# One plain channel pair fewer ahead of the seven-product stage of a gated conv-MLP, and a weight ring that begins at another place

## The chip, the cores and the metric

One Trainium2 chip, of which the kernel uses one core. The metric is the device time of one launch in microseconds (us), the median of repeated runs; lower is better. Everything is float32.

## What is computed

A decoder layer on x (1, 1024, 1024): a mixer half, which the change does not touch, and a channel mixer:

```python
h  = rms_norm(x, norm_ffn_pre)                                   # (1024 tokens, 1024)
up = causal_dwconv(h @ w_up, conv_w, taps=3) + conv_b            # w_up: 1024 x 5632
gate, val = split(up, 2)                                         # 2816 channels each
x  = x + rms_norm((silu(gate) * val) @ w_down, norm_ffn_post)    # w_down: 2816 x 1024
```

The 2816 channels are 22 tiles of 128. A *pair* is one tile of gate channels with the tile of value channels of the same number.

## The kernel before, in words

Every float32 product is made of three TensorE matmuls on rounded parts (`product`, L1438 to L1444): high times high, high times low, low times high. So each operand is first rounded by ScalarE into a high part and then subtracted by VectorE into a low part. h transposed lies in `h2hi` and `h2lo` (8 token tiles by 8 k tiles).

Pairs are made in two ways. In a **plain** pair the gate and the value tile are each multiplied with both halves of the tokens: 2 x 2 x 8 k tiles x 3 = 96 matmuls of 512 columns (the loop at L1663). In a **seven-product** pair the same result comes from 7 products (Strassen's scheme with Winograd's sums) over quarters of h and of the pair's weights, each 4 k tiles x 3 = 12 matmuls, together 84 (`seventh`, L1670; the loop over q at L1682). `PLAIN = 3` pairs are plain, and the 19 others (`SEVEN`) are seven-product pairs, q = 0 to 18 for pairs 3 to 21.

The seven products of pair q are here called P1 to P7, in the order in which TensorE issues them. They need:
- the **differences** of h's quarters, four arrays of 128x2048 that are made once. GpSimd adds high and low parts to whole quarters (`whole_quarter`, L581); VectorE combines them (L1331, L1335, L1336, L1343); ScalarE rounds (`round_difference(i)`, L842); VectorE takes the low part (`low_difference(i)`, L1299). P2, P3, P5 and P7 read the differences 0, 1, 2 and 3 (`r_split` counts them).
- the weight **entries** (q, 0) to (q, 3), per pair: raw blocks or sums of them. GpSimd makes the sums (`sum_weights`, L586, three instructions, after the low part of entry (q-1, 2)), ScalarE rounds (`round_entry`, L848), VectorE takes the low part (`low_entry`, L1305, counted by `u_split`). P1 and P4 read entry 0, P2 and P5 entry 1, P3 and P6 entry 2, P7 entry 3.
- copies and additions of partial products: ScalarE copies the results of P1, P2 and P3 out of PSUM (`keep(q, 0..2)`, L867), since P3 adds onto the bank of P1 and P5 onto that of P3; VectorE adds them elsewhere (`fold(q, 0..2)`, L1318), and P7 waits for the second of these.

After its products a pair is convolved: ScalarE starts gate and value (`start_gate`, `start_value`), VectorE adds the taps (`gate_taps`, `value_taps`, two instructions each), ScalarE takes SiLU, VectorE multiplies (`gate_value`).

Entries go round a **ring** of six places (`entry`, L358): two in `w2hi`/`w2lo`, two in a quarter of `h2hi`/`h2lo` that only plain pairs and the differences read, two in `whi`/`wlo`, which the plain pairs' weights use before. Entries (0, 2) and (0, 3) lie in the h2 quarter, so they wait until all plain pairs are done (L853 and L854).

No planner sets the order: each engine runs its own program in the order in which the code is written. ScalarE's order around the change is at L900 to L931, VectorE's at L1329 to L1370, TensorE's at L1663 to L1703, GpSimd's at L605 to L610, and SyncE's, which loads weights and stores results, at L488 to L491: `load_pair(p)` waits for two `w_split` if pair p-2 is plain, otherwise for the four `u_split` of pair p-2, and `save_act(p-3)` follows it in the same queue.

Of the kernel before, what the change touches and what calls it, by code (L numbers as in the profile page):

```python
# [21 lines left out]
ACT = mybir.ActivationFunctionType  # L22
# [11 lines left out]
NF = DFF // P  # L34
# [13 lines left out]
UP0 = W_O0 + KD  # L48
# [13 lines left out]

PLAIN = 3
SEVEN = NF - PLAIN
W_SPLIT_DOWN = UP0 + 2 * PLAIN
RING = 6

ENTRY_LAST = (4, 5, 6, 7)  # L70


def build(nc, consts, x, norm_mix_pre, w_in, pool_w, pool_scale, conv_w, attn_sinks, w_o,
# [10 lines left out]
    with ctx:  # L84
# [20 lines left out]
        whi = alloc(ctx, "whi", [P, SPLIT, DM], F32R)  # L105
# [18 lines left out]
        h2hi = alloc(h2, "h2hi", [P, NT, KD, P], F32R)  # L124
        h2lo = alloc(h2, "h2lo", [P, NT, KD, P], F32R)
# [58 lines left out]
        w2hi = alloc(x2_, "w2hi", [P, 2, DM], F32R)  # L184
        w2lo = alloc(x2_, "w2lo", [P, 2, DM], F32R)
        w_sums = alloc(x2_, "w_sums", [P, 4, HALF])
        yg = alloc(x2_, "yg", [P, 2, SEQ])
        yv = alloc(x2_, "yv", [P, 2, SEQ])
# [16 lines left out]
        def banks(b, n=2):  # L205
            return ps[:, b:b + n, :].rearrange("p b c -> p (b c)")
# [16 lines left out]
        def ffn_tap(j, f):  # L223

            return par_b[:, bass.ds(f, 1)] if j == 2 else par_a[:, bass.ds(2 * NF * j + f, 1)]

        def ffn_bias(f):
            return par_b[:, bass.ds(2 * NF + f, 1)]
# [13 lines left out]
        act_saved = [sem("act_saved0"), sem("act_saved1")]  # L242
# [56 lines left out]
        up_done = sem("up_done")  # L299
        neg_ready = sem("neg_bias_ready")  # L300
        quartered = sem("h2_quarters_added")
# [9 lines left out]
        yg_started = sem("gate_started")  # L311
        yv_started = sem("value_started")
        silu_done = sem("silu_done")
        up_freed = sem("up_convolved")
        act_ready = sem("act_ready")
# [41 lines left out]

        def entry(q, i, lo):  # L358

            at = (4 * q + i) % RING  # L360
            if at < 2:
                return (w2lo if lo else w2hi)[:, at, :].rearrange("p (h c) -> p h c", h=2)
            if at < 4:
                t = 4 + 2 * (at - 2)
                return (h2lo if lo else h2hi)[:, t:t + 2, 0:4, :].rearrange("p t k c -> p t (k c)")
            return (wlo if lo else whi)[:, at - 4, :].rearrange("p (h c) -> p h c", h=2)

        def raw_blocks(pair):
# [10 lines left out]
        def _(sp):  # L379
# [39 lines left out]
            def load_pair(p):  # L419
                for val in range(2):  # L420
                    n = UP0 + 2 * p + val
                    if p - 2 < PLAIN:
                        sp.wait_ge(w_split, n - RAW + 1)
# [132 lines left out]
        def _(pool):  # L556
# [29 lines left out]
            def sum_weights(q):  # L586

                pair = PLAIN + q
                raw = raw_blocks(pair)
# [38 lines left out]
        def _(act):  # L628
            def round_weight(base, q, hi, slot):

                n = base + RAW * q
                act.wait_ge(landed[base % RAW], 16 * (base // RAW + 1 + q))
                act.activation(hi[:, slot, :], wraw[:, base % RAW, :], ACT.Copy)\  # L633
                   .then_inc(w_rounded, 1)
# [180 lines left out]
                    round_ring(UP0 + t - 4)  # L815
            round_h(2 * NT - 1, h2hi)

            def plain_step(p):

                j = p % 2  # L820
                act.wait_ge(up_done, 2 * p + 1)
                if p + 1 < PLAIN:
                    round_weight(UP0 + 2 * p + 2, 0, whi, 0)
                if p >= 2:
                    act.wait_ge(act_ready, p - 1)
                act.activation(yg[:, j, :], banks(4 * j), ACT.Identity, bias=ffn_bias(p),
                               scale=ffn_tap(2, p)).then_inc(yg_started, 1)
                act.wait_ge(up_done, 2 * p + 2)
                if p + 1 < PLAIN:
                    round_weight(UP0 + 2 * p + 3, 0, whi, 1)  # L830
                if p >= 2:
                    act.wait_ge(act_saved[j], 16 * (p // 2))
                act.activation(yv[:, j, :], banks(4 * j + 2), ACT.Identity,
                               bias=ffn_bias(p + NF), scale=ffn_tap(2, p + NF))\
                   .then_inc(yv_started, 1)
                start_silu(p)

            def start_silu(p):
                act.wait_ge(up_freed, 2 * p + 1)
                act.activation(yg[:, p % 2, :], yg[:, p % 2, :], ACT.Silu).then_inc(silu_done, 1)  # L840

            def round_difference(i):  # L842
                act.wait_ge(r_made, i + 1)
                act.activation(r_hi[i][:, :, :, :].rearrange("p t k c -> p (t k c)"),
                               r_full[i][:, :, :].rearrange("p t c -> p (t c)"),
                               ACT.Copy).then_inc(r_rounded, 1)

            def round_entry(q, i):  # L848
                pair = PLAIN + q
                before = 4 * q + i - RING  # L850
                if before >= 0:
                    act.wait_ge(seven_done, 7 * (before // 4) + ENTRY_LAST[before % 4])
                elif (4 * q + i) % RING >= 2:  # L853
                    act.wait_ge(up_done, 2 * PLAIN)  # L854
                if i in (0, 3):
                    n = UP0 + 2 * pair + (i == 3)
                    act.wait_ge(landed[n % RAW], 16 * (n // RAW + 1))
                    raw = raw_blocks(pair)
                    src = raw[:, 0:2, :] if i == 0 else raw[:, 3:4, :]
                else:  # L860
                    act.wait_ge(summed, 3 * q + (1 if i == 1 else 3))
                    src = w_sums[:, 0:2, :] if i == 1 else w_sums[:, 2:4, :]
                out = entry(q, i, False)
                act.activation(out[:, 0:1, :] if i == 3 else out, src, ACT.Copy)\
                   .then_inc(u_rounded, 1)
# [31 lines left out]
            for q in x2_saved:  # L897
                act.wait_ge(q, 16 * NT // 2)
            act.wait_ge(neg_ready, 1)
            plain_step(0)  # L900
            plain_step(1)
            round_difference(0)
            round_entry(0, 0)
            round_entry(0, 1)
            round_difference(1)
            plain_step(2)
            round_difference(2)
            round_entry(0, 2)
            round_entry(0, 3)
            round_difference(3)  # L910
            for q in range(SEVEN):
                if q >= 1:
                    start_value(q - 1)
# [64 lines left out]
        def _(dve):  # L978
# [261 lines left out]
            for t in range(NT):  # L1240
                rows = x2b[:, t % 2, :]
                i = NT + 2 * t
# [29 lines left out]
            def gate_taps(p):  # L1272
                dve.wait_ge(yg_started, p + 1)
                add_taps(yg[:, p % 2, :], banks(4 * (p % 2)), p)

            def value_taps(p):
                dve.wait_ge(yv_started, p + 1)
                add_taps(yv[:, p % 2, :], banks(4 * (p % 2) + 2), p + NF)

            def gate_value(p, sign):  # L1280

                dve.wait_ge(up_freed, 2 * p + 2)
                dve.wait_ge(silu_done, p + 1)
                dve.scalar_tensor_tensor(yv[:, p % 2, :], yv[:, p % 2, :], sign, yg[:, p % 2, :],
                                         ALU.mult, ALU.mult).then_inc(act_ready, 1)

            def plain_step(p):
                if p + 1 < PLAIN:
                    low_weight(UP0 + 2 * p + 2, 0, whi, wlo, 0)
                gate_taps(p)  # L1290
                if p + 1 < PLAIN:
                    low_weight(UP0 + 2 * p + 3, 0, whi, wlo, 1)
                value_taps(p)
                gate_value(p, 1.0)
# [4 lines left out]
            def low_difference(i):  # L1299
                dve.wait_ge(r_rounded, i + 1)  # L1300
                dve.tensor_tensor(r_lo[i][:, :, :, :].rearrange("p t k c -> p t (k c)"), made(i),
                                  r_hi[i][:, :, :, :].rearrange("p t k c -> p t (k c)"),
                                  ALU.subtract).then_inc(r_split, 1)

            def low_entry(q, i):  # L1305
                dve.wait_ge(u_rounded, 4 * q + i + 1)
                hi, lo = entry(q, i, False), entry(q, i, True)
                raw = raw_blocks(PLAIN + q)
                if i == 0:
                    src = raw[:, 0:2, :]  # L1310
                elif i == 3:
                    src, hi, lo = raw[:, 3:4, :], hi[:, 0:1, :], lo[:, 0:1, :]
                else:
                    dve.wait_ge(summed, 3 * q + 3)
                    src = w_sums[:, 2 * i - 2:2 * i, :]
                dve.tensor_tensor(lo, src, hi, ALU.subtract).then_inc(u_split, 1)  # L1316
# [12 lines left out]
            plain_step(0)  # L1329
            dve.wait_ge(quartered, 2)  # L1330
            dve.tensor_tensor(made(0), made(0), made(2), ALU.subtract).then_inc(r_made, 1)  # L1331
            plain_step(1)
            dve.wait_ge(r_made, 1)
            dve.wait_ge(quartered, 3)
            finish_step(dve.tensor_tensor(made(2), made(1), made(2), ALU.subtract))  # L1335
# [7 lines left out]
            dve.scalar_tensor_tensor(made(3), made(1), -1.0, made(3), ALU.mult, ALU.subtract)\  # L1343
               .then_inc(r_made, 2)
            low_difference(1)
            plain_step(2)
            low_difference(2)
            low_entry(0, 2)
            low_entry(0, 3)
            low_difference(3)  # L1350
            for q in range(SEVEN):
                if q >= 1:
                    value_taps(PLAIN + q - 1)
# [61 lines left out]
            for t in range(4):  # L1415
                i, slot = 3 * NT + 4 + t, t % 2
# [373 lines left out]
```

## Time and profile before

| | |
|---|---|
| median of 3 runs | 1002.41 us (999.76 to 1004.15) |
| the profiled execution, its own time | 1003.03 us |
| its span in the trace | 1001.2 us |
| mean granted TensorE clock | 0.994 of full |
| TensorE (PE) busy | 983.2 us, 98% |
| VectorE (DVE) busy | 613.3 us, 61% |
| ScalarE (ACT) busy | 407.8 us, 41% |
| GpSimd (POOL) busy | 158.2 us, 16% |

Times in the rows are microseconds from the start of the span. A row of a timeline gives the start, the duration, the engine, the line of the kernel, the operation, what it writes and reads with its shape, and how many instructions are merged; in square brackets stands how long the engine had been idle before, and which instruction released it. A matmul's duration includes its way through the array, so matmuls overlap; what counts is the distance between their starts. L1441 to L1443 are the three matmuls of every product. A helper's line serves many calls: L1301 is every `low_difference`, L1316 every `low_entry`, L1326 every `fold`, L1262 and L1264 the taps, L864 every `round_entry`, L844 every `round_difference`, L877 every `keep`.

### The profile page before, as it was taken

Reading aid. Unit: us, or ns where it says so; the run is one execution under the profiler, and the core shown is the slowest. Engines: PE = TensorE matmul, PEld = TensorE weight load, DVE = VectorE, ACT = ScalarE, POOL = GpSimd, SP = SyncE. Lnnn points to the kernel's source line nnn. Section 1 sums busy time; section 2 is a strip of 40 time slices with the busy share of each in tenths; the row PEclk is TensorE's granted clock in tenths of the full one; section 3 lists DMA queues with packets and bytes.
Section 4 is the critical chain, followed back from the end, with each engine's and each line's share of the span. In section 5 each row is a group of like instructions: output and inputs, shape, how many; then the busy total and the mean of one; then the engine's idle time right before and its main releaser. Section 6 shows DMA issues by size and latency. Waiting matters only on the chain.

```text
span 1001.2 us, 11938 instructions
## 1 busy us (share of the span) xinstructions
PE 983.2 (98%) x4580; PEld 810.0 (81%) x4580; DVE 613.3 (61%) x641; ACT 407.8 (41%) x624; POOL 158.2 (16%) x143
## 2 busy tenths in 40 slices
PE   8999999999999998999999999999999999999997
PEld 7988777777888887888888888888887888888886
DVE  4646786664555579777677677677665333344454
ACT  5525444443343335444445445445433323333342
POOL 2200000000111832332242232232200000000001
PEclk9999999999999999999999999999999999999999
DMA  6511110016223321232223223223315444455553
GB/s 221 154 49 37 43 43 22 25 61 209 85 85 104 86 84 47 80 93 86 75 79 90 84 66 102 85 64 105 105 64 191 155 139 144 157 191 197 182 175 126
DMA packets 84911, 104.90 MB, mean 105 GB/s; under 512 B 3849, under 2 KB 63489, under 8 KB 84865
## 3 DMA queue, kind: packets, MB, share of 16 engines
q1 hardware_dynamic: 84737, 104.20, 31.9%
q8 instruction: 31, 0.51, 0.2%
q14 instruction: 15, 0.12, 0.0%
q0 software_dynamic: 128, 0.07, 0.0%
HBM read 84.33 MB, written 19.92 MB: 104 GB/s over the span
## 4 chain that ended last, share of the span: by engine, by line
PE 91%; DVE 3%; DMA 2%; ACT 1%; POOL 1%; issue 1%; SPq 0%; DVEq 0%; POOLq 0%; ACTq 0%
PE ps L1441 29%; PE ps L1442 29%; PE ps L1443 29%; PE ps L1451 1%; PE ps L1549 1%; PE ps L1572 1%; DMA wraw<-in_w_in 1%; PE ps L1550 1%; PE ps L1558 1%; PE ps L1576 1%; DMA wraw<-in_w_o 1%; DMA act_in<-act_dram 0%; DVE hlo L992 0%; PE ps L1587 0%; DVE w2lo L1316 0%
## 5 line engine op out<-in xcount | busy, mean ns | idle before, releaser
L992 DVE TENSOR_TENSOR wlo<-wraw,whi 128x1024 fp32r<-128x1024 f32 x60 | 75.8, 1265 | 138.1 <-ACT whi L633 137.8
L633 ACT ACTIVATE whi<-wraw 128x1024 fp32r<-128x1024 f32 x60 | 63.4, 1058 | 173.4 <-PE ps L1443 169.3
L1441 PE MATMUL ps<-whi,ahi 128*128 128x512 f32 x320 | 124.6, 389 | 1.6 <-DVE alo L1269 1.6
L1443 PE MATMUL ps<-whi,alo 128*128 128x512 f32 x320 | 124.5, 389 | 0.0
L1442 PE MATMUL ps<-wlo,ahi 128*128 128x512 f32 x320 | 124.5, 389 | 0.0
L1441 PE MATMUL ps<-hhi,whi 128*128 128x512 f32 (+1 forms) x256 | 96.4, 376 | 2.3 <-DVE hlo L1010 2.3
L1442 PE MATMUL ps<-hlo,whi 128*128 128x512 f32 (+1 forms) x256 | 93.7, 366 | 0.0
L1443 PE MATMUL ps<-hhi,wlo 128*128 128x512 f32 (+1 forms) x256 | 93.7, 366 | 0.0
L563 POOL TENSOR_SCALAR meansq<-sumsq 128x1 f32<-128x1 f32 x28 | 7.6, 272 | 526.7 <-ACT x2b L804 241.7
L595 POOL TENSOR_TENSOR w_sums<-wraw 128x1024 f32<-128x1024 f32 x19 | 46.7, 2459 | 255.2 <-DVE h2lo L1316 103.4
L1441 PEld LDWEIGHTS ps<-whi,ahi 128*128 128x128 f32 x320 | 60.1, 188 | 14.4 <-DVE alo L1269 2.0
L1443 PEld LDWEIGHTS ps<-whi,alo 128*128 128x128 f32 x320 | 60.1, 188 | 12.6
L1442 PEld LDWEIGHTS ps<-wlo,ahi 128*128 128x128 f32 x320 | 60.1, 188 | 12.4
L1441 PE MATMUL ps<-h2hi,whi 128*128 128x512 f32 x168 | 65.5, 390 | 0.0
L1442 PE MATMUL ps<-h2lo,whi 128*128 128x512 f32 x168 | 65.4, 389 | 0.0
L1443 PE MATMUL ps<-h2hi,wlo 128*128 128x512 f32 x168 | 65.4, 389 | 0.0
L1441 PEld LDWEIGHTS ps<-hhi,whi 128*128 128x128 f32 x256 | 49.1, 192 | 10.0 <-DVE hlo L1010 2.7
L1443 PEld LDWEIGHTS ps<-hhi,wlo 128*128 128x128 f32 x256 | 49.1, 192 | 7.6
L1442 PEld LDWEIGHTS ps<-hlo,whi 128*128 128x128 f32 x256 | 49.1, 192 | 7.4 <-issue 0.5
L1441 PE MATMUL ps<-hhi,mhi 128*128 128x512 f32 x128 | 51.3, 401 | 2.2 <-DVE hlo L992 2.2
L1442 PE MATMUL ps<-hlo,mhi 128*128 128x512 f32 x128 | 50.6, 395 | 0.0
L1443 PE MATMUL ps<-hhi,mlo 128*128 128x512 f32 x128 | 50.5, 394 | 0.0
(196 smaller groups left out, 2215.8 us busy)
## 6 DMA issues: line engine op xcount, KB each, us to landing
wraw<-in_ffn_w_up SPq DMA_DIRECT2D x44, 512.0 KB, 5.1
wraw<-in_ffn_w_down SPq DMA_DIRECT2D x44, 512.0 KB, 3.4
act_dram<-yv SPq DMA_DIRECT2D x22, 512.0 KB, 2.6
act_in<-act_dram SPq DMA_DIRECT2D x42, 256.0 KB, 3.5
wraw<-in_w_in SPq DMA_DIRECT2D x14, 512.0 KB, 4.0
xin<-in_x SPq DMA_DIRECT2D x8, 512.0 KB, 4.3
wraw<-in_w_o SPq DMA_DIRECT2D x8, 512.0 KB, 3.3
xres<-in_x SPq DMA_DIRECT2D x8, 512.0 KB, 4.2
```

What stands on the lines that cost most here:

```text
L595: pool.tensor_tensor(w_sums[:, 0:2, :], raw[:, 0:4:3, :], raw[:, 2:3, :].broadcast_to([P, 2, HALF]), ALU.add)\
L633: act.activation(hi[:, slot, :], wraw[:, base % RAW, :], ACT.Copy)\
L992: dve.tensor_tensor(lo[:, slot, :], wraw[:, base % RAW, :], hi[:, slot, :], ALU.subtract).then_inc(w_split, 1)
L1441: pe.matmul(acc, w_hi, x_hi, start=first, stop=False, skip_group_check=looped)
L1442: pe.matmul(acc, w_hi, x_lo, start=False, stop=False, skip_group_check=looped)
L1443: return pe.matmul(acc, w_lo, x_hi, start=False, stop=last, skip_group_check=looped)
L1451: last = pe.transpose(ps[:, b + k // 4, (k % 4) * P:(k % 4 + 1) * P], rows[:, k * P:(k + 1) * P], ident)
L1549: pe.matmul(acc, q, k_hi[:, kv, keys], start=True, stop=False)
L1550: last = pe.matmul(acc, q, k_lo[:, kv, keys], start=False, stop=True)
L1558: last = pe.transpose(ps[:, 6, i * P:(i + 1) * P], prob[:, u % 2, i, :], ident)
L1572: last = pe.matmul(acc, v_tok[:, b, cols], pt_cur[:, heads, :].rearrange("p h q -> p (h q)"), start=True, stop=b == 0)
L1576: last = pe.matmul(acc, v_tok[:, b - 1, cols], pt_prev[:, heads, :].rearrange("p h q -> p (h q)"), start=False, stop=True)
```

## The change

`PLAIN` goes from 3 to 2, so pair 2 becomes a seven-product pair and q runs from 0 to 19, for pairs 2 to 21. The ring is entered at its third place (`RING_FROM = 2`), and the names of the first two pairs of places are exchanged: entries (0, 0) and (0, 1) still lie in `w2`, (0, 2) and (0, 3) now in `whi`/`wlo`, and the first to lie in the h2 quarter are (1, 0) and (1, 1). Entry (0, 2) waits for the first three of the plain pairs' four tiles, entry (0, 3) for all four, those of q = 1 also for the whole quarters. ScalarE's and VectorE's programs around the transition are written in another order: the work of the last plain pair (now pair 1) is split up and put among the differences and entries.

```diff
-PLAIN = 3
+PLAIN = 2
 SEVEN = NF - PLAIN
 W_SPLIT_DOWN = UP0 + 2 * PLAIN
 RING = 6
+RING_FROM = 2
@@ def entry(q, i, lo)
-            at = (4 * q + i) % RING
+            at = (4 * q + i + RING_FROM) % RING
             if at < 2:
-                return (w2lo if lo else w2hi)[:, at, :].rearrange("p (h c) -> p h c", h=2)
+                t = 4 + 2 * at
+                return (h2lo if lo else h2hi)[:, t:t + 2, 0:4, :].rearrange("p t k c -> p t (k c)")
             if at < 4:
-                t = 4 + 2 * (at - 2)
-                return (h2lo if lo else h2hi)[:, t:t + 2, 0:4, :].rearrange("p t k c -> p t (k c)")
+                return (w2lo if lo else w2hi)[:, at - 2, :].rearrange("p (h c) -> p h c", h=2)
@@ ScalarE: plain_step(p) becomes start_plain(p, val), one half of it, and start_silu(p)
+            def start_plain(p, val):
+                j, y = p % 2, (yg, yv)[val]
+                act.wait_ge(up_done, 2 * p + val + 1)
                 if p + 1 < PLAIN:
-                    round_weight(UP0 + 2 * p + 2, 0, whi, 0)
...
+                    round_weight(UP0 + 2 * p + 2 + val, 0, whi, val)
+                act.activation(y[:, j, :], banks(4 * j + 2 * val), ACT.Identity,
+                               bias=ffn_bias(p + val * NF), scale=ffn_tap(2, p + val * NF))\
+                   .then_inc((yg_started, yv_started)[val], 1)
@@ def round_entry(q, i)
-                elif (4 * q + i) % RING >= 2:
-                    act.wait_ge(up_done, 2 * PLAIN)
+                elif 4 * q + i >= 2:
+                    act.wait_ge(up_done, 2 * PLAIN - (4 * q + i == 2))
+                    if 4 * q + i >= 4:
+                        act.wait_ge(quartered, 2)
@@ ScalarE, the order
-            plain_step(0)
-            plain_step(1)
+            start_plain(0, 0)
+            start_plain(0, 1)
+            start_silu(0)
             round_difference(0)
             round_entry(0, 0)
             round_entry(0, 1)
             round_difference(1)
-            plain_step(2)
             round_difference(2)
+            start_plain(1, 0)
             round_entry(0, 2)
+            round_difference(3)
+            start_plain(1, 1)
             round_entry(0, 3)
-            round_difference(3)
+            start_silu(1)
@@ VectorE, the order
             plain_step(0)
             dve.wait_ge(quartered, 2)
             dve.tensor_tensor(made(0), made(0), made(2), ALU.subtract).then_inc(r_made, 1)
-            plain_step(1)
...
             low_difference(1)
-            plain_step(2)
+            gate_taps(1)
             low_difference(2)
             low_entry(0, 2)
+            low_difference(3)
             low_entry(0, 3)
-            low_difference(3)
+            value_taps(1)
+            gate_value(1, 1.0)
```

## Rows read from the trace of the kernel before

**Rows 1.** The page, the chain that ended last: shares of the span by engine.

```profile
PE 91%; DVE 3%; DMA 2%; ACT 1%; POOL 1%; issue 1%; SPq 0%; DVEq 0%; POOLq 0%; ACTq 0%
```

**Rows 2.** Timeline of PE: pair 1's end, products of q = 0, two of q = 1.

```profile
364.35 0.39 PE L1441 MATMUL ps<-h2hi,whi 128*128 128x512 f32 x1
...
386.11 0.39 PE L1441 MATMUL ps<-h2hi,w2hi 128*128 128x512 f32 x1
...
395.05 0.77 PE L1441 MATMUL ps<-r_hi,h2hi 128*128 128x512 f32 x1 [3.35 <-ACT yg L877]
...
399.47 0.39 PE L1441 MATMUL ps<-h2hi,w2hi 128*128 128x512 f32 x1
...
410.38 0.39 PE L1441 MATMUL ps<-h2hi,whi 128*128 128x512 f32 x1
...
416.41 0.50 PE L1441 MATMUL ps<-r_hi,w2hi 128*128 128x512 f32 x1 [0.43 <-ACT yg L877]
```

**Rows 3.** Busy time by stretch, q = 0: stretch, length, PE, PEld, DVE, ACT, POOL, clock, DMA.

```profile
386.11:410.38 24.27, 20.92 (x86) 16.89 (x84) 21.46 (x15) 12.77 (x14) 12.00 (x5) 0.93 0.22 66
```

**Rows 4.** Timeline of DVE, from the first difference to the folds of q = 0.

```profile
355.87 2.30 DVE L992 TENSOR_TENSOR wlo<-wraw,whi 128x1024 fp32r<-128x1024 f32 x1
...
372.87 2.29 DVE L1336 SCALAR_TENSOR_TENSOR r_full<-r_full 128x2048 f32<-128x2048 f32 x1
375.08 2.28 DVE L1301 TENSOR_TENSOR r_lo<-r_full,r_hi 128x2048 fp32r<-128x2048 f32 x1
377.28 1.22 DVE L1316 TENSOR_TENSOR w2lo<-wraw,w2hi 128x1024 fp32r<-128x1024 f32 x1
...
379.55 2.28 DVE L1343 SCALAR_TENSOR_TENSOR r_full<-r_full 128x2048 f32<-128x2048 f32 x1
381.75 2.28 DVE L1301 TENSOR_TENSOR r_lo<-r_full,r_hi 128x2048 fp32r<-128x2048 f32 x1
383.96 1.27 DVE L1262 SCALAR_TENSOR_TENSOR yg<-ps,par_a,yg 128x1023 f32<-128x1023 f32 x1
...
390.18 1.22 DVE L1284 SCALAR_TENSOR_TENSOR yv<-yv,yg 128x1024 f32<-128x1024 f32 x1
...
395.26 4.45 DVE L1301 TENSOR_TENSOR r_lo<-r_full,r_hi 128x2048 fp32r<-128x2048 f32 x1
...
404.95 1.22 DVE L1316 TENSOR_TENSOR w2lo<-w_sums,w2hi 128x1024 fp32r<-128x1024 f32 x1
...
406.69 2.60 DVE L1316 TENSOR_TENSOR w2lo<-wraw,w2hi 128x512 fp32r<-128x512 f32 x1
409.21 0.69 DVE L1326 TENSOR_TENSOR ps<-ps,yv 128x512 f32<-128x512 f32 x1
```

**Rows 5.** Timeline of POOL: weight sums of q = 0, 1 and 2.

```profile
353.87 3.22 POOL L599 TENSOR_TENSOR w_sums<-w_sums,wraw 128x512 f32<-128x512 f32 x1
357.17 2.16 POOL L602 TENSOR_TENSOR w_sums<-w_sums,wraw 128x512 f32<-128x512 f32 x1
394.91 2.66 POOL L595 TENSOR_TENSOR w_sums<-wraw 128x1024 f32<-128x1024 f32 x1 [35.58 <-DVE h2lo L1316]
...
406.34 2.40 POOL L595 TENSOR_TENSOR w_sums<-wraw 128x1024 f32<-128x1024 f32 x1 [3.23 <-DVE w2lo L1316]
408.82 1.62 POOL L599 TENSOR_TENSOR w_sums<-w_sums,wraw 128x512 f32<-128x512 f32 x1
```

**Rows 6.** Timeline of ACT: one of each kind of instruction at the transition.

```profile
375.20 1.92 ACT L844 ACTIVATE r_hi<-r_full 128x2048 fp32r<-128x2048 f32 x1 [3.85 <-DVE r_full L1336]
377.02 1.19 ACT L826 ACTIVATE yg<-ps,par_b 128x1024 f32<-128x1024 f32 x1
...
390.17 1.04 ACT L864 ACTIVATE h2hi<-w_sums 128x1024 fp32r<-128x1024 f32 x1
391.11 0.62 ACT L864 ACTIVATE h2hi<-wraw 128x512 fp32r<-128x512 f32 x1
...
394.38 1.06 ACT L877 ACTIVATE yg<-ps 128x512 f32<-128x512 f32 x2
```

**Rows 7.** DMA issues, 380 to 440: queue, KB each, median us to landing.

```profile
wraw<-in_ffn_w_up SPq DMA_DIRECT2D x6, 512.0 KB, 4.8
```

More of the change, by code:

```diff
@@ L816, in _ @@
             round_h(2 * NT - 1, h2hi)
-            def plain_step(p):
-                j = p % 2
-                act.wait_ge(up_done, 2 * p + 1)
+            def start_plain(p, val):
+                j, y = p % 2, (yg, yv)[val]
+                act.wait_ge(up_done, 2 * p + val + 1)
                 if p + 1 < PLAIN:
-                    round_weight(UP0 + 2 * p + 2, 0, whi, 0)
[L824 to L836, printed above, removed]
+                    round_weight(UP0 + 2 * p + 2 + val, 0, whi, val)
+                act.activation(y[:, j, :], banks(4 * j + 2 * val), ACT.Identity,
+                               bias=ffn_bias(p + val * NF), scale=ffn_tap(2, p + val * NF))\
+                   .then_inc((yg_started, yv_started)[val], 1)
             def start_silu(p):
```

## The prediction

> **What bounds the kernel now.** I read the chain that ended last first: TensorE holds 91% of it [rows 1], so a removed matmul is time saved, unless TensorE then waits. Next comes its timeline for the places where it does wait [rows 2]. From 399.47 (P4 of q = 0) to 410.38 (P1 of q = 1) lie 48 matmuls with no gap: 0.2273 us apiece, so 12 take 2.73 us, a seven-product pair 19.1, a plain pair 21.8. The transition is not at this pace: q = 0 takes 24.27 us, P3 starts only at 395.05 after 3.35 us idle, released by a ScalarE copy, and P3 of q = 1 starts at 416.41 where 24 matmuls after 410.38 would give 415.84. From 386.11 to 416.41 are 30.3 us for 108 matmuls that need 24.55, a loss of 5.75 us. The 12 matmuls of P3 after the idle time take 4.42 us in place of 2.73, as the granted clock of this stretch is 0.93 [rows 3]: part of it ran at 1.2 GHz, not 2.4. Last I read VectorE, GpSimd and ScalarE there [rows 4 to 6], because they decide when P3 may go. After 416.41 TensorE shows no other gap until the down stage, so it suffices to ask when P3 of q = 1 starts, with the other engines in the same positions behind it.
>
> **What it removes.** One plain pair becomes a seven-product pair, 96 to 84 matmuls: -2.73 us. That holds if the transition loses as much as today. Behind P3 of q = 1 the changed kernel has one pair more than before, 19.1 us, so its time is (its start of that P3) - 416.41 + 19.1. Equal time needs that start at 397.3.
>
> **What it moves.** Pair 1 ends at 364.35 [rows 2]; P1 of q = 0 could start there, 21.8 us earlier than today. But the differences and entries do not come 21.8 us earlier: VectorE, ScalarE and GpSimd have the same work to do with one plain pair less as cover. I follow VectorE from 355.87, where the first difference has been made and today a low weight of pair 2 starts [rows 4]; up to there nothing changes.
>
> VectorE and GpSimd take turns. GpSimd's L599 at 353.87 takes 3.22 us where the one at 408.82 takes 1.62, and VectorE's 512-column entry at 406.69 lasts 2.60 us and ends when GpSimd's L595 (406.34 + 2.40) has gone by plus about 0.6 [rows 4, 5]: one waits for the other's whole instruction.
> - The two combinations L1335 and L1336 (2.2 us from start to start, 372.87 to 375.08) now come at 355.87. The first waits for GpSimd's L599 to 357.1 and ends at 359.2; GpSimd's last sum (about 1.3 alone) goes to 360.4, the second combination ends at 362.55.
> - Low difference 0 (2.2), entries (0, 0) and (0, 1) (1.14 each), L1343 (2.2), low difference 1 (2.2) by the pitches of rows 4: entry (0, 0) is ready at 365.9, (0, 1) at 367.0, the last combination at 369.2, low difference 1 at 371.4. So P1 starts at 366.0 instead of 364.35, P2 follows, and both end at 371.4.
> - ScalarE waits for the last combination (369.2) before difference 2 (1.9) [rows 6], then starts the gate of pair 1 (1.2): 372.3. Behind it are queued entry (0, 2) (1.0), difference 3 (1.9), the value of pair 1 (1.2), entry (0, 3) (0.6), SiLU (taken as 1.0, the same size as an entry), entry (1, 0) (1.0) and only then keep (0, 0) (0.6), which ends at 379.0. P3 waits for it.
> - VectorE: gate taps 372.3 to 374.9 (2.6: two of 1.3), low difference 2 to 377.1, entry (0, 2) ready at 378.25, which P3 needs too. P3 therefore starts at 379.1, after 7.7 us of idle time; today that is 3.35.
> - Low difference 3 issues at 378.17, just ahead of GpSimd's L595 for the next pair (it waits for entry (0, 2)), and should take 2.3, not the 4.45 of the row at 395.26, whose turn came after a short entry had let GpSimd in. Then GpSimd 380.4 to 382.7, entry (0, 3) to 383.3, value taps to 385.8, and the product of gate and value waits for GpSimd's third sum and ends at 387.3 (alone 1.22). Entries (1, 0) and (1, 1) to 389.6, fold 0 to 390.2, entry (1, 2) from 390.1, fold 1 until 392.0, entry (1, 3) behind GpSimd's L595, fold 2 at 394.4 (4.26 after entry (1, 2) started, as from 404.95 to 409.21).
> - TensorE meanwhile: P3 at the slow pace to 383.5, P4, P5, P6 to 391.7, P7 waits for fold 1 to 392.0, P1 and P2 of q = 1 would be done at 400.2.
> - From fold 2 to P3 of q = 1 it is 7.2 us today (409.21 to 416.41: gate start, taps, SiLU, entry, keep). 394.4 + 7.2 = 401.6. That P3 waits 1.4 us.
>
> **The sum.** 401.6 - 416.41 + 19.1 = +4.3; unrounded it is +4.2. By losses: 1.6 (P1) + 7.7 (P3) + 1.7 (clock) + 0.3 (P7) + 1.4 (next P3), with rounding 12.6 against 5.75 today, less the 2.73. 1003.03 + 4.2 = 1007.2 for the profiled execution; that one lies 0.6 above the median 1002.41, so I forecast 1006.6. A measurement of this kernel can tell about 0.5%, 5.0 us, from no change: this is +0.42%.
>
> **At nothing.** The ring's new order alone: the places have the same size and the instructions that use them the same shape; with 20 pairs the last users of `whi` are again the third and fourth entries of the last but one pair, so the down stage starts as now. Its cover, if the places were wrong, would be a wait of each entry for a product 6 entries back; steady pairs show no such wait on TensorE, and the distance is unchanged. SyncE's queue: `load_pair(4)` now waits for entry (0, 3) (383.3) and holds back the store of pair 1, ready at 387.3 anyway. Its two loads land 4.8 us after issue [rows 7], about 389.3, ahead of GpSimd's 391.4; nobody needs the sum before 400. The half clock after P3's idle time costs nothing beyond the 1.7, as P7 and the next P3 wait for VectorE anyway; without it the time would be the same.
>
> **The unknown: who takes a turn.** Low difference 3 beside GpSimd: 2.3 at least (it is ahead), 4.45 at most (the row at 395.26). At 4.45 GpSimd's second sum also goes ahead of entry (0, 3), which is ready at 385.0; the product follows at 388.75 in place of 387.3, so everything behind is 1.45 later: +5.7. I take 2.3, because the issue order differs from that row's. The first combination has 2.3 and 4.48 as ends (its neighbour before 355.87 ran twice its time beside GpSimd), I have 3.4: 1.1 either way.
>
> A rule speaks to this. The Trainium skill (SBUF — State Buffer, Who interferes with whom) says that whichever engine issues first holds the shared pair of ports for its whole instruction. By it low difference 3 goes first and the result is +4.2; by the nearest row it would be +5.7. The 512-column entry of 2.60 agrees with a lock and not with sharing, which would about double its time to 1.3.
>
> **Rivals.**
> (a) *VectorE loses its turns and the transition costs more* (slower side). Place: low difference 3, then the product and entry (1, 3). Price +1.45, together +5.7, 1008.1; it decides if GpSimd's L595 is issued before low difference 3 starts, a margin of 0.2 us. For it: that is what happened at 395.26. Against: the order there. A wait on ScalarE's list of seven items ahead of keep (0, 0) can add to it. Chance 0.30.
> (b) *The transition loses no more than today*: P3's 3.35 us, the slow 12 matmuls. Then -2.73, 999.7. It needs VectorE's chain 7 us shorter than I follow it. For: three instruction groups of pair 2's plain work are gone. Against: they are not in the chain above. Chance 0.06.
> (c) *All waits vanish*, -2.73 - 5.75 = -8.5, 993.9: only if keep (0, 0) came by 371. Chance 0.05.
> (d) *TensorE stays at 1.2 GHz* after the longer idle time up to P3 of q = 1: 84 matmuls at 4.42/12 = 0.368 from 379.1 give 410.0, +12.7, 1015.1. For it only that the idle time doubles; the 12 matmuls after 395.05 were back at full pace by P4. Chance 0.03.
> (The Trainium skill, TensorE: Matmul & The Clock Gate, HAM oscillation, describes kernels that swing between the two levels when matmul groups are spaced by waits; that would be (d).)
> That the change does not do what it says has no room here: the counts are constants.
>
> **How the numbers follow.** Forecast +4.2: chance 0.56, within 0.5%. Faster by over 0.5%: (c), 0.05. Slower: (a) and (d), 0.33. Within: the forecast and (b), 0.62. The range goes 5 us below the forecast, to 1001.5, for a shorter first combination and the scatter of the runs (999.76 to 1004.15), and up to 1010.5, which takes in (a) with the same scatter. It leaves out (b), (c), (d).
>
> **What the changed trace would show.** 12 matmuls fewer, 4568 in place of 4580. P1 of q = 0 about 1.6 us after pair 1's end, then P3 7 to 8 us late, released by a keep on ScalarE then a half-pace stretch of 12 matmuls; a fold ahead of P7; P3 of q = 1 near 401.6. VectorE without idle time over 1.2 us between 355.9 and 395. Low difference 3 of 2.3 us would confirm the turn taken, 4.45 would give (a). I would be wrong if P3 started before 375, or if a gap appeared on TensorE later than 402, which none of this accounts for.

## The result, and the profile after

The changed kernel took 1005.91 us (median of 9 runs, 1004.79 to 1008.31) against 1002.02 us for the one before in the same session (9 runs, 999.76 to 1004.33). The ratio is 1.0040, 95% interval 1.0029 to 1.0052: slower by 0.4%, 3.9 us of the medians, less than the 0.5% that was named as the bound of "no change". The forecast was +4.2 us and 1006.6 us.

The page of the changed kernel, span and busy time by engine:

```profile
span 1003.3 us, 11939 instructions
PE 979.1 (98%) x4568; PEld 806.1 (80%) x4568; DVE 618.6 (62%) x646; ACT 412.3 (41%) x629; POOL 163.6 (16%) x146
```

There are 4568 matmuls, 12 fewer than before, and TensorE is 4.1 us less busy, yet the span is 2.1 us longer. The two spans cannot be compared directly. Both kernels are the same up to the last transposes of the mixer half, and that point lies at different times in different executions. So I use the start of those eight transposes as a **mark** for all traces. Timelines of PE, before and after, the mark:

```profile
326.69 1.06 PE L1451 MATMUL ps<-cst,hrow_c 128*128 128x128 f32 x8 [0.51 <-DVE hrow_c L1254]
```

```profile
325.21 1.06 PE L1449 MATMUL ps<-cst,hrow_c 128*128 128x128 f32 x8 [0.52 <-DVE hrow_c L1251]
```

The execution shown of the changed kernel had been 1.48 us quicker to that point. Timeline of PE of the changed kernel at the transition: P1 and P3 of q = 0, P4 of q = 0, P1 and P3 of q = 1:

```profile
364.56 0.47 PE L1439 MATMUL ps<-h2hi,w2hi 128*128 128x512 f32 x1 [1.53 <-DVE w2lo L1313]
...
377.64 0.77 PE L1439 MATMUL ps<-r_hi,whi 128*128 128x512 f32 x1 [7.36 <-ACT yg L871]
...
382.11 0.39 PE L1439 MATMUL ps<-h2hi,w2hi 128*128 128x512 f32 x1
...
393.05 0.39 PE L1439 MATMUL ps<-h2hi 128*128 128x512 f32 x1
...
399.77 0.50 PE L1439 MATMUL ps<-r_hi,w2hi 128*128 128x512 f32 x1 [1.12 <-ACT yg L871]
```

These are the rows that answer to [rows 2]. From the mark to P3 of q = 1 it is 74.56 us; before it was 89.72. One more pair of 19.04 us follows (the distance of the folds of two steady pairs, 84 matmuls at 0.2267), so the transition accounts for 74.56 + 19.04 - 89.72 = +3.9 us, the size of the difference of the medians. From the mark to the end of the span it is 678.1 us against 674.5 before, +3.6: the only other wait of TensorE until there that differs is the one at the start of the down stage, 1.32 us in place of 1.62. TensorE idles 1.5 us ahead of P1, 7.4 ahead of P3 and 1.1 ahead of the next P3, and P3's 12 matmuls take 4.47 us. P7 starts at 390.26, 65.05 us after the mark, right behind P6 and 0.1 us after fold 1 has ended (389.45 + 0.69). Busy time by stretch of the changed kernel (columns as in [rows 3]), around P3:

```profile
377.60:382.10 4.50, 4.46 (x12) 3.56 (x13) 4.50 (x3) 0.43 (x1) 4.42 (x2) 0.60 0.01 4
```

The granted clock is 0.60 there: most of it ran at 1.2 GHz.

### VectorE and GpSimd after

Timeline of DVE of the changed kernel, from the first of the two combinations to fold 2 of q = 0, to be read beside [rows 4]:

```profile
354.51 3.27 DVE L1331 TENSOR_TENSOR r_full<-r_full 128x2048 f32<-128x2048 f32 x1
357.82 3.27 DVE L1332 SCALAR_TENSOR_TENSOR r_full<-r_full 128x2048 f32<-128x2048 f32 x1
...
370.84 1.28 DVE L1259 SCALAR_TENSOR_TENSOR yg<-ps,par_a,yg 128x1023 f32<-128x1023 f32 x1 [0.88 <-ACT yg L826]
...
375.56 1.22 DVE L1313 TENSOR_TENSOR wlo<-w_sums,whi 128x1024 fp32r<-128x1024 f32 x1
376.69 2.29 DVE L1298 TENSOR_TENSOR r_lo<-r_full,r_hi 128x2048 fp32r<-128x2048 f32 x1
378.89 2.87 DVE L1313 TENSOR_TENSOR wlo<-wraw,whi 128x512 fp32r<-128x512 f32 x1
...
389.45 0.69 DVE L1323 TENSOR_TENSOR ps<-ps,yg 128x512 f32<-128x512 f32 x1
390.05 2.59 DVE L1313 TENSOR_TENSOR w2lo<-wraw,w2hi 128x512 fp32r<-128x512 f32 x1
392.56 0.69 DVE L1323 TENSOR_TENSOR ps<-ps,yv 128x512 f32<-128x512 f32 x1
```

Timeline of POOL of the changed kernel, the third sum of q = 0 and the first of q = 1:

```profile
355.71 3.22 POOL L603 TENSOR_TENSOR w_sums<-w_sums,wraw 128x512 f32<-128x512 f32 x1
376.94 4.27 POOL L596 TENSOR_TENSOR w_sums<-wraw 128x1024 f32<-128x1024 f32 x1 [18.01 <-DVE wlo L1313]
```

VectorE has one idle time, 0.88 us, in 38 us. The turns can be read off: GpSimd's sum issued at 355.71 (1.3 us alone) gets its turn when VectorE's combination has ended at 357.8, and ends 1.15 us later; VectorE's next combination takes 3.27 us, not 2.29, because that sum is ahead of it. Low difference 3, issued at 376.69, takes 2.29: it is ahead of GpSimd's sum of 376.94, which takes 4.27 instead of 2.39, and entry (0, 3) behind both takes 2.87 instead of 0.7. That decides between the two prices of the prediction: the turn was taken, not lost.

### The profile page after: what moved, and what is told of

Its sections match the earlier page's. It is cut to its first block, busy times and chain, and to the rows that moved or that the text cites. A ratio compares the mean times of both kernels' runs of the same rounds, so it can differ in the third digit from the quotient of the medians.

```text
span 1003.3 us, 11939 instructions
## 1 busy us (share of the span) xinstructions
PE 979.1 (98%) x4568; PEld 806.1 (80%) x4568; DVE 618.6 (62%) x646; ACT 412.3 (41%) x629; POOL 163.6 (16%) x146
## 4 chain that ended last, share of the span: by engine, by line
PE 89%; DVE 6%; DMA 2%; ACT 1%; issue 1%; SPq 0%; POOL 0%; DVEq 0%; POOLq 0%; ACTq 0%
PE ps L1439 28%; PE ps L1441 28%; PE ps L1440 28%; PE ps L1449 1%; PE ps L1547 1%; PE ps L1570 1%; DMA wraw<-in_w_in 1%; PE ps L1548 1%; PE ps L1556 1%; DVE r_lo L1298 1%; PE ps L1574 1%; DMA wraw<-in_w_o 1%; DVE w2lo L1313 0%; DMA act_in<-act_dram 0%; DVE r_full L1328 0%
## 5 line engine op out<-in xcount | busy, mean ns | idle before, releaser
L989 DVE TENSOR_TENSOR wlo<-wraw,whi 128x1024 fp32r<-128x1024 f32 x58 | 72.4, 1249 | 133.1 <-ACT whi L634 132.8
L634 ACT ACTIVATE whi<-wraw 128x1024 fp32r<-128x1024 f32 x58 | 61.3, 1059 | 159.0 <-PE ps L1441 154.1
L596 POOL TENSOR_TENSOR w_sums<-wraw 128x1024 f32<-128x1024 f32 x20 | 50.7, 2537 | 253.4 <-DVE wlo L1313 99.4
L1440 PEld LDWEIGHTS ps<-wlo,ahi 128*128 128x128 f32 x320 | 60.1, 188 | 12.4
L1439 PE MATMUL ps<-h2hi,whi 128*128 128x512 f32 x140 | 54.6, 390 | 0.0
L1440 PE MATMUL ps<-h2lo,whi 128*128 128x512 f32 x140 | 54.5, 389 | 0.0
L1441 PE MATMUL ps<-h2hi,wlo 128*128 128x512 f32 x140 | 54.5, 389 | 0.0
```

What stands on the lines that cost most here:

```text
L596: pool.tensor_tensor(w_sums[:, 0:2, :], raw[:, 0:4:3, :], raw[:, 2:3, :].broadcast_to([P, 2, HALF]), ALU.add)\
L989: dve.tensor_tensor(lo[:, slot, :], wraw[:, base % RAW, :], hi[:, slot, :], ALU.subtract).then_inc(w_split, 1)
L1439: pe.matmul(acc, w_hi, x_hi, start=first, stop=False, skip_group_check=looped)
L1440: pe.matmul(acc, w_hi, x_lo, start=False, stop=False, skip_group_check=looped)
L1441: return pe.matmul(acc, w_lo, x_hi, start=False, stop=last, skip_group_check=looped)
```

## The experiments

Each is told by three numbers: the distance from the mark to P3 of q = 0 and to P3 of q = 1, and the ratio to the kernel before with its interval. With two plain pairs, 19.04 us are added before it is compared with three. The edits are shown shortened, some of them in words.

| kernel | mark to P3, q = 0 | mark to P3, q = 1 | ratio | median, us |
|---|---|---|---|---|
| before | 68.36 | 89.72 | 1 | 1001.5 to 1003.0 by session |
| changed | 52.43 | 74.56 | 1.0040 [1.0029, 1.0052] | 1005.91 |
| e1, ring of before | 52.41 | 74.55 | 1.0036 [1.0022, 1.0050] | 1005.24 |
| e2, keep (0, 0) earlier | 51.69 | 74.52 | 1.0039 [1.0025, 1.0053] | 1005.90 |
| e3, VectorE longer | 52.41 | 76.91 | 1.0057 [1.0038, 1.0075] | 1007.72 |
| e4, filler matmuls | 52.38 | 74.55 | 1.0040 [1.0025, 1.0054] | 1005.95 |
| e5, quarters on VectorE | 45.60 | 67.72 | 0.9967 [0.9953, 0.9981] | 999.02 |
| e6, reordered | no gap | 65.45 | 0.9950 [0.9932, 0.9968] | 998.49 |
| e7, folds first | no gap | 62.13 | 0.9914 [0.9889, 0.9938] | 993.56 |
| e10, the same again | no gap | 62.13 | 0.9896 [0.9874, 0.9918] | 992.49 |
| e8, three plain, quarters on VectorE | 68.37 | 89.71 | 0.9983 [0.9971, 0.9995] | 1001.15 |
| e11, the same again | 68.36 | 89.71 | 1.0003 [0.9988, 1.0018] | 1003.44 |
| e9, three plain, clean | 65.54 | 84.69 | 0.9933 [0.9913, 0.9953] | 996.30 |
| e12, changed again | 52.42 | 74.54 | 1.0054 [1.0035, 1.0073] | 1007.79 |

### Does the ring's order cost anything?

```diff
-RING_FROM = 2
+RING_FROM = 0
 places 0, 1: w2; places 2, 3: the h2 quarter; places 4, 5: whi/wlo
 entries (0, 2), (0, 3): wait for all plain tiles and two whole quarters
 first down weights: wait for P4 and P5 of the last pair
```

> The changed kernel with the ring of the kernel before (first two places in w2, then the h2 quarter, then whi/wlo), so entries (0, 2) and (0, 3) lie in the h2 quarter and wait for all four plain tiles; the first down weights then wait for P4 and P5 of the last pair. Theory (the loss is VectorE's and ScalarE's chain at the transition, the ring's order costs nothing): P3 of q = 0 and P3 of q = 1 within 0.3 us of the changed kernel's 377.6 and 399.8, total within noise of its 1005.9, +3.9 to before. Rival (the ring's order is part of the loss): total 2 us or more below the changed kernel's.

P3 of q = 1 comes 74.55 us after the mark, 0.01 us from the changed kernel. The ring's order costs nothing at this transition: entries (0, 2) and (0, 3) were late anyway. At the end of the stage it leaves a wait of 0.30 us on TensorE at 753.54 that the changed kernel does not have.

### Is it the queue ahead of keep (0, 0)?

```diff
             round_difference(3)
+            keep(0, 0)
             start_plain(1, 1)
...
-                for which in range(3):
+                for which in range(q == 0, 3):
```

> The changed kernel with keep (0, 0) moved ahead of the value start of pair 1 on ScalarE, past four instructions. Theory (VectorE's chain up to fold 2 sets the time, TensorE's idle time ahead of P3 does not): P3 of q = 0 starts 0.8 us earlier, 376.8 in place of 377.6, now released by entry (0, 2); P3 of q = 1 stays at 399.8 and the total at +3.9 to before. Rival (the queue ahead of the copy is the cost): P3 of q = 1 and the total come earlier by the same 0.8 us or more.

Timeline of PE, P3 of q = 0 and of q = 1:

```profile
378.70 0.77 PE L1440 MATMUL ps<-r_hi,whi 128*128 128x512 f32 x1 [6.63 <-DVE wlo L1314]
...
401.53 0.50 PE L1440 MATMUL ps<-r_hi,w2hi 128*128 128x512 f32 x1 [0.81 <-ACT yg L871]
```

P3 is now released by VectorE's entry and comes 0.74 us earlier (51.69 after the mark). P3 of q = 1 comes 0.04 us earlier. Idle time ahead of P3 was shortened and the kernel did not get faster: the copy that the profile names as releaser is not what sets the time. The fair comparison is e12 below, the changed kernel in an execution in which P3's 12 matmuls took 5.3 us as they did here: of the 0.73 us gained ahead of P3, 0.66 came back as idle time ahead of the next P3 (0.81 us against 0.15).

### Is it VectorE's chain?

```diff
             value_taps(1)
+            for _ in range(2):
+                finish_step(dve.tensor_tensor(gain_a[:, :], banks(4), h2lo_tile_0, ALU.add))
             gate_value(1, 1.0)
```

> The changed kernel with two more VectorE instructions of 128x1024 (about 1.3 us each, one input in PSUM, result not used) between the value taps of pair 1 and its product, so after P3 of q = 0 has been released. Theory (VectorE's chain from there to fold 2 sets the time): P3 of q = 0 stays at 377.6, P7 of q = 0 and P3 of q = 1 come 2.6 us later, total +6.5 to before. Rival (what counts is TensorE's idle time ahead of P3): +3.9 as now, the 2.6 us lie beside TensorE's work.

Timelines of DVE and PE: the added pair, then P3 and P7 of q = 0 and P3 of q = 1:

```profile
384.40 2.47 DVE L1349 TENSOR_TENSOR gain_a<-ps,h2lo 128x1024 f32<-128x1024 f32 x2
```

```profile
377.86 0.77 PE L1443 MATMUL ps<-r_hi,whi 128*128 128x512 f32 x1 [7.38 <-ACT yg L871]
...
392.85 0.47 PE L1443 MATMUL ps<-r_hi,whi 128*128 128x512 f32 x1 [1.51 <-issue]
...
402.36 0.50 PE L1443 MATMUL ps<-r_hi,w2hi 128*128 128x512 f32 x1 [1.09 <-ACT yg L871]
```

The two instructions took 2.5 us, P3 of q = 0 stayed (52.41), and P3 of q = 1 came 2.35 us later, with P7 now waiting 1.5 us. The profile names no releaser for P7 ("issue"), but P7 starts 0.10 us after fold 1 has ended (392.06 + 0.69 on VectorE), and it is the same 0.10 us in e4 and e6. Time added to VectorE behind P3's release goes into the total almost in full. The measured ratio, 1.0057, has the changed kernel's within its interval, so here the trace shows it and the median only leans that way.

### Is it the half clock?

```diff
+                if q == 0:
+                    for _ in range(30):
+                        pe.matmul(bank g0, a weight of entry (0, 0), h2hi quarter, start=True, stop=True)
                 pe.wait_ge(kept, 3 * q + 1)
```

> The changed kernel with 30 matmuls of 512 columns whose result is overwritten, between P2 and P3 of q = 0: 6.8 us of work in the idle time, so that the granted clock does not fall. Theory: P3 takes 2.7 us in place of 4.5, but P7 still waits for fold 1 on VectorE and P3 of q = 1 for the copy, so the total stays at +3.9 to before (within 0.4). Rival (the half clock is part of the loss): total 1.7 us below the changed kernel's, +2.2 to before.

Timelines of PE and DVE: the fillers, P3 and P7 of q = 0, P3 of q = 1, then fold 1:

```profile
372.53 7.00 PE L1692 MATMUL ps<-h2hi,w2hi 128*128 128x512 f32 x30
...
379.99 0.50 PE L1439 MATMUL ps<-r_hi,whi 128*128 128x512 f32 x1 [0.46 <-ACT yg L871]
...
392.65 0.47 PE L1439 MATMUL ps<-r_hi,whi 128*128 128x512 f32 x1 [1.48 <-issue]
...
402.16 0.50 PE L1439 MATMUL ps<-r_hi,w2hi 128*128 128x512 f32 x1 [1.11 <-ACT yg L871]
```

```profile
391.86 0.69 DVE L1323 TENSOR_TENSOR ps<-ps,yg 128x512 f32<-128x512 f32 x1
```

P3's 12 matmuls ran at full pace (2.86 us in place of 4.47), and what they gained turned into the 1.48 us that P7 waits for fold 1. P7 starts 65.04 us after the mark, P3 of q = 1 74.55, both where they were. In e12, the changed kernel once more, the half clock lasted longer: the 12 matmuls of P3 took 5.3 us, and P3 of q = 1 was again at 74.54 with only 0.15 us of idle time ahead of it. So the half clock was free here, but with little to spare:

```profile
380.08 0.76 PE L1439 MATMUL ps<-r_hi,whi 128*128 128x512 f32 x1 [7.36 <-ACT yg L871]
...
402.20 0.50 PE L1439 MATMUL ps<-r_hi,w2hi 128*128 128x512 f32 x1 [0.15 <-ACT yg L871]
```

> The changed kernel itself beside the three others: ratio 1.004 to before.

Its ratio, 1.0054, has an interval from 1.0035 that overlaps the first, so +4 to +5.5 us is what the ratios of two sessions give (the medians of this one lie 6.2 us apart). The two traces agree within 0.3 us from the mark to the end of the span (678.3 and 678.1), so the rest is not at the transition; where it comes from is open.

One number joins the three tests: from the start of fold 2 to P3 of q = 1 it is 7.19 to 7.21 us in the kernel before, in the changed one and in e1 to e6 and e12, whatever TensorE does in between.

### Shortening the chain: the quarters on VectorE

```diff
 GpSimd
-            for i, out in ((0, 0), (3, 2), (2, 1), (1, 3)):
-                whole_quarter(i, out)
+            pool.wait_ge(quartered, 4)
 VectorE, ahead of plain_step(0)
+            dve.wait_ge(ht_split, 2 * NT)
+            dve.wait_ge(wo_done, NT)
+            for i, out in ((0, 0), (3, 2), (2, 1), (1, 3)):
+                whole_quarter(i, out)
```

> The changed kernel with the four whole quarters added by VectorE (four instructions of 128x2048, 2.2 us each, in its idle time from 328.6 on) and not by GpSimd, whose weight sums begin behind them; every order otherwise as in the changed kernel. Theory: the instructions after the first difference come 6.8 us earlier (second combination done at 354.3 in place of 361.1), P1 of q = 0 follows pair 1 with no gap at 362.9, P3 starts at 370.9 after some 2.5 us idle, P3 of q = 1 at 393.0; total 6.8 us below the changed kernel's, 2.9 below before (ratio 0.997). Rival (ScalarE's queue or the waits for up_done set the time): P3 of q = 1 moves by less than 3 us.

Timeline of DVE, the four quarters, and of PE, both P3:

```profile
328.19 8.90 DVE L1323 TENSOR_TENSOR r_full<-h2hi,h2lo 128x2048 f32<-128x2048 f32 x4
```

```profile
370.36 0.47 PE L1442 MATMUL ps<-r_hi,whi 128*128 128x512 f32 x1 [2.34 <-ACT yg L865]
...
392.48 0.50 PE L1442 MATMUL ps<-r_hi,w2hi 128*128 128x512 f32 x1 [1.09 <-ACT yg L865]
```

Four quarters took 8.9 us on VectorE, in idle time; in the kernel before, GpSimd took 20.3 us for them and held up VectorE's instructions of the first plain pair. The Trainium skill (GPSIMD Engine Reference, Elementwise — side-by-side cycle accounting) gives 4497 against 2293 ns for an add of 2048 float32 elements per partition; here VectorE's took 2.29 us each, and GpSimd's 4.60 for the first, beside which VectorE was idle (328.61 to 337.12 in the changed kernel), and up to 5.6 for the later ones, beside a working VectorE. The trace agrees with the page within some 2%. P1 follows pair 1 without a gap, P3 of q = 1 is 6.84 us earlier than in the changed kernel (expected 6.8), and the ratio is 0.9967.

### Reordering for the deadlines

```diff
 VectorE (e6)
+ made(0) between the gate and value work of pair 0
+ low_entry(0, 0), made(3), low_difference(0), low_entry(0, 1), low_difference(1), low_entry(0, 2),
+ gate_taps(1), value_taps(1), low_entry(0, 3), low_difference(2), low_difference(3), gate_value(1)
 ScalarE (e6)
+ ... start_plain(1, 0), round_entry(0, 2), round_difference(2), round_difference(3),
+ start_plain(1, 1), round_entry(0, 3), keep(0, 0), start_silu(1)
 VectorE (e7), q = 0, in place of the loop's order
+ fold(0, 0), gate_value(1), fold(0, 1), low_entry(1, 0), low_entry(1, 1), fold(0, 2),
+ low_entry(1, 2), gate_taps(2), low_entry(1, 3)
 ScalarE (e7): keep(1, 0) ahead of start_silu(2)
```

> As the quarters on VectorE, and both engines' programs reordered up to the loop over q: VectorE makes all differences first, takes entry (0, 2) before and low differences 2 and 3 after the taps of pair 1; ScalarE copies keep (0, 0) ahead of SiLU of pair 1. Theory: P1, P2 and P3 of q = 0 follow pair 1 with no gap (P3 at 368.3), P7 waits 2.7 us for fold 1 on VectorE, P3 of q = 1 starts at 391.6; total 8.2 us below the changed kernel's, 4.3 below before (0.996). Rival (P3's idle time is the cost, so that removing it brings all): P3 of q = 1 at 388, 12 us below the changed kernel's.

Timeline of PE of e6, P7 of q = 0 and P3 of q = 1:

```profile
383.17 0.47 PE L1447 MATMUL ps<-r_hi,whi 128*128 128x512 f32 x1 [1.79 <-issue]
...
392.69 0.50 PE L1447 MATMUL ps<-r_hi,w2hi 128*128 128x512 f32 x1 [1.09 <-ACT yg L865]
```

P3's idle time is gone and, as the theory had it, that alone is not all: P7 waits 1.8 us (expected 2.7) and the next P3 1.1. P3 of q = 1 is 9.1 us earlier than in the changed kernel, where 8.2 was expected and 12 by the rival.

> As the reordered kernel, and at q = 0 VectorE does fold 0 ahead of the product of pair 1, fold 1 ahead of entry (1, 0), fold 2 ahead of entry (1, 2) and the gate taps ahead of entry (1, 3); ScalarE does keep (1, 0) ahead of the SiLU of pair 2. Theory: no wait of TensorE is left from pair 1 to P3 of q = 1 at 387.4, the loss of the transition is below 1 us, total 12 us below the changed kernel's and 8.5 below before, 993.5 (ratio 0.9915). If only part of the waits goes, what is left shows as a gap ahead of P7 or P3.

Timeline of PE of e7, P1 of q = 0 and P3 of q = 1, and its busy time by stretch:

```profile
362.50 0.39 PE L1457 MATMUL ps<-h2hi,w2hi 128*128 128x512 f32 x1
...
386.98 0.39 PE L1457 MATMUL ps<-r_hi,w2hi 128*128 128x512 f32 x1
```

```profile
330.00:362.00 32.00, 32.00 (x143) 26.50 (x142) 31.86 (x19) 17.70 (x14) 7.70 (x3) 1.00 0.16 50
362.00:381.00 19.00, 19.00 (x85) 15.73 (x85) 18.93 (x16) 9.07 (x12) 5.01 (x3) 1.00 0.27 84
```

24.48 us for 108 matmuls, 0.2267 apiece: no loss is left, the clock stays at 1.00, and TensorE is busy without a break while VectorE is busy 18.93 of 19 us. 993.56 us, ratio 0.9914 where 0.9915 was expected; again with more rounds:

> The kernel with the folds first once more, with more rounds: ratio 0.9915 to before, 8.5 us below, and 12.4 us below the changed kernel timed beside it.

992.49 us, 0.9896 [0.9874, 0.9918]. This version beats both kernels. It lies below the one before by 8.6 us by the traces, by 9.4 and 9.1 us by the medians of the two sessions, and by 8.6 and 10.4 by their ratios.

### Three plain pairs with the same treatment

> The kernel before (three plain pairs) with the quarters added by VectorE in the same way, its orders otherwise kept. Theory: there P3 of q = 0 is released by ScalarE's copy, which stands in its queue behind everything that follows pair 2's end at 386.1, and none of that waits for the differences; so P3 stays 3.4 us idle and the total is that of before within 0.5 us (ratio 1.000). Rival (late differences are what cost there as well): P3 and the total 3 us earlier or more.

Only the quarters' move, applied to the kernel before. Both P3 are where they were, to 0.01 us, but the ratio of 0.9983 was not explained by that. Hence the repetition:

> The kernel before with only the quarters moved to VectorE once more, since its first ratio of 0.9983 was 1.8 us lower than its trace explains. Theory (the transition is unchanged): ratio 0.9995, within 0.1% of 1. Rival (the quarters on VectorE gain time elsewhere): 0.998 again.

1.0003, and from the mark to the end of the span both executions take 0.2 us less than the kernel before (674.3 and 674.4 against 674.5). So the first ratio is put down to scatter, and an interval that leaves out 1 by 0.05% is no proof of a gain. The loss of the changed kernel rests on firmer ground: e1, e2, e4 and e12 all show it again. With three plain pairs VectorE's late quarters are covered, and P3 waits for ScalarE's copy alone.

```diff
 the kernel before, quarters on VectorE, and at the transition
 ScalarE: gate start of pair 2, differences 2 and 3, entry (0, 2), value start, entry (0, 3), keep(0, 0), SiLU
 VectorE: gate_taps(2), low_difference(2), low_difference(3), low_entry(0, 2), value_taps(2),
          low_entry(0, 3), then the folds as in e7
```

> Three plain pairs and the ring of before, with the quarters on VectorE and both engines' programs reordered at the transition in the manner of the kernel with the folds first. Theory (with no wait at the transition the seven-product pair is worth its 12 matmuls): no gap on TensorE from pair 2 to P3 of q = 1, total 5.8 us below before (ratio 0.994) and 2.7 us above the same with two plain pairs. Rival (plain pairs and seven-product pairs differ by more than their matmuls): any other distance to that kernel than 2 to 3.5 us.

Timelines of PE (P3 of q = 0), of ACT (rounding of entry (0, 2)) and of DVE (low differences 2 and 3, then the low part of that entry):

```profile
390.60 0.47 PE L1465 MATMUL ps<-r_hi,h2hi 128*128 128x512 f32 x1 [0.53 <-DVE h2lo L1321]
```

```profile
384.67 1.06 ACT L858 ACTIVATE h2hi<-w_sums 128x1024 fp32r<-128x1024 f32 x1 [0.71 <-PE ps L1467]
```

```profile
384.83 4.48 DVE L1306 TENSOR_TENSOR r_lo<-r_full,r_hi 128x2048 fp32r<-128x2048 f32 x2
389.24 1.22 DVE L1321 TENSOR_TENSOR h2lo<-w_sums,h2hi 128x1024 fp32r<-128x1024 f32 x1
```

Three plain pairs lose 0.8 us at this transition (25.28 us for the 108 matmuls), and P3 waits for entry (0, 2). Two things come together there. The entry lies in the h2 quarter, so ScalarE rounds it only after pair 2 has ended, at 384.67. And its low part stands in VectorE's program behind low differences 2 and 3, which P3 does not need, and so starts at 389.24. One low difference takes 2.2 us, so with the entry between the two it would by estimate have been ready at 388.2, ahead of the 389.9 at which P2 ends, and P3 would have had no wait in the old ring either; no run tries it. By the traces two plain pairs are 84.69 - 62.13 - 19.04 = 3.5 us better, 2.7 for the 12 matmuls and 0.8 for this wait; by the medians 3.8 in the same session, just outside the 2 to 3.5 us that the expectation allowed, and 2.7 against e7. The expectation of no gap failed by this one wait, and whether the new ring order has any worth of its own is not shown.

## Why the prediction was right

**The saving**, -2.73 us for 12 matmuls: right. It follows from the pace, 12 x 0.2267 us, and of the 3.5 us between the traces of e9 and e7 it is what remains when e9's loss of 0.8 is taken off.

**VectorE's chain from 355.87**: right to some tenths. With 1.48 us added for the earlier mark, the second combination ended at 362.6 (predicted 362.55), P3 of q = 0 started at 379.1 (379.1), low difference 3 took 2.29 us (2.3), fold 2 issued at 394.0 (394.4), P3 of q = 1 started at 401.25 (401.6). The 0.4 us too much came from the product of pair 1, for which I had it wait for GpSimd's third sum; that sum had ended by then. For the same reason P7 did not wait for a fold, as I had said the trace would show: fold 1 ended 0.1 us ahead of it, and the 0.3 us priced for it did not appear. The loss of the transition was 12.4 us against 12.6. That the median came out within 0.7 us of the forecast is in part luck: the changed kernel's own median moved by 1.9 us from one session to the other.

**Which wait counts.** The prediction had both TensorE's idle time ahead of P3 and VectorE's chain to fold 2 in one list of losses, though it said that the half clock costs nothing because the later waits are VectorE's. That was right and the list invites the wrong reading: e2 shortened the largest entry of it and nothing came of it, e4 removed the 1.7 us and P7 waited instead. Each loss on TensorE is real time, but in this kernel the sum of them is fixed by VectorE's chain to fold 2 and the 7.2 us behind it.

**Rival (a)**, lost turns, +5.7: the trace speaks against it, the turn was taken. Its price cannot be seen. **(b)** and **(c)**, no more waits than today: wrong for this change, and both to be had with other orders: e5 and e7 lie at -3.0 and -8.6 us by the traces, as (b) and (c) had priced them (-2.7 and -8.5). **(d)**, the clock staying low: after 7.4 us of idle time it was at 1.2 GHz for some 3.6 us in one execution and 5.7 in another (below), not to the end.

**At nothing**: the ring's order (e1) cost nothing, as said. SyncE's loads did not show as a wait of TensorE anywhere after the mark.

## What to carry to other kernels

A block of independent work is also cover for what must be ready after it. Before shortening it, add up the engines that prepare the next stage and compare with what is left; here 21.8 us of cover went for 2.7 us of matmuls. Follow the chain past the largest gap: the releaser named at the gap (a ScalarE copy) could be moved without effect, and what counted was the engine without idle time. And give setup work to an engine in its idle time rather than to a slower one that shares its turns: this turned +3.9 us into -3.0, and ordering by deadline into -8.6.

## What the runs showed of the hardware

- The length of the half-clock stretch after the same idle time of 7.36 to 7.38 us was not the same: P3's 12 matmuls took 4.47 us in the changed kernel's first trace and 5.25, 5.26 and 5.11 in e12, e1 and e3, 2.73 at full pace. Over the first 8.2 us from P3 the granted clock was 0.78 in the first and 0.65 in e12, so with the two levels it was at 1.2 GHz for 2 x 0.22 x 8.2 = 3.6 us and 2 x 0.35 x 8.2 = 5.7 us. P3 of q = 1 started 74.56, 74.54 and 74.55 us after the mark in the first, e12 and e1.
- VectorE and GpSimd alternate by whole instructions with both inputs in SBUF, in every row looked at (2.29 us alone, 3.27 or 4.48 behind a GpSimd instruction for 2048 elements); which was issued first decided, and predicted, the durations worked out here to about 0.1 us. Taps that read PSUM kept their 1.27 to 1.28 us beside GpSimd.
- The mark itself scatters by 2.9 us (324.76 to 327.66) between executions of programs that are alike up to it, as much as the effect studied. Distances from it to the same event agreed to 0.02 us between sessions, where medians of whole runs needed repetition.
